# Last two expert blocks of a mixture-of-experts layer held in PSUM: sum rows added by identity products, normalised rows scattered to the outputs

## The reference, cut to what matters

```
def layer(x, ...):
    h = rmsnorm(x, g_mix); z = h @ w_in
    ...                                     # pool and retention branches
    x = x + mixed @ w_out
    h2 = rmsnorm(x, g_ffn)
    return x + hier_moe(h2, w_grp, w_exp, w1, w3, w2)

def hier_moe(h, ...):
    # a group of 8 experts by the largest group logit; in it the 2 best experts
    # weight = p_group * softmax of the two logits
    # per expert:  a = silu(xb @ w1[e]) * (xb @ w3[e]);  y = (a @ w2[e]) * weight
    # y is added to the row of its token

y_prompt, y_sample = rmsnorm(yp, g_final), rmsnorm(ys, g_final)
```

## Time and profile before

| | |
|---|---|
| Median of 3 runs | 1022.72 us (1022.17 to 1023.6) |
| The profiled execution | 1020.73 us, its span 1019.0 us |
| PE busy | 965.6 us (95%) |
| DVE, ACT, POOL busy | 740.3 us, 443.9 us, 219.4 us |
| Chain that ended last | PE 86%, DVE 6%, DMA 4% |
| First expert product, last expert product | at 684.0 us and at 987.5 us |

### The profile page before, as it was taken

The page is one execution under the profiler, slowest core; times in us unless marked ns, Lnnn a source line. Parts: engine busy times, 40 slices in busy tenths (PEclk is TensorE's granted clock), DMA queues, the critical chain, the costliest instruction groups (busy, mean ns, idle before and its releaser), DMA issues.

```text
span 1019.0 us, 16208 instructions
## 1 busy us (share of the span) xinstructions
PE 965.6 (95%) x5356; PEld 835.9 (82%) x5357; DVE 740.3 (73%) x1631; ACT 443.9 (44%) x739; POOL 219.4 (22%) x225
## 2 busy tenths in 40 slices
PE   6999999999999999999999999969999999999970
PEld 6998898988889888898886888857888888888860
DVE  5965466855678556685558666589999999999965
ACT  6621122121221212212113112148988998898864
POOL 0001220012200122001221100031443443443220
PEclk9999999999999999999999999979999999999995
DMA  9511105111051110512027332389999999999938
GB/s 317 179 42 54 42 22 176 40 53 39 25 173 41 54 34 29 173 33 80 35 81 261 150 140 103 117 310 408 394 393 393 391 401 388 392 395 382 340 50 333
DMA packets 74627, 190.21 MB, mean 187 GB/s; under 512 B 12519, under 2 KB 47443, under 8 KB 62131
## 3 DMA queue, kind: packets, MB, share of 16 engines
q1 hardware_dynamic: 61099, 159.07, 41.1%
q0 software_dynamic: 13312, 29.69, 9.9%
q10 hardware_dynamic: 144, 0.52, 0.2%
HBM read 167.43 MB, written 38.68 MB: 202 GB/s over the span
## 4 chain that ended last, share of the span: by engine, by line
PE 86%; DVE 6%; DMA 4%; ACT 1%; issue 1%; SPq 0%; POOL 0%; DVEq 0%; POOLq 0%; ACTq 0%
PE bank L2007 17%; PE bank L887 12%; PE bank L889 12%; PE bank L888 11%; PE bank L2008 9%; PE bank L918 8%; PE bank L1058 3%; PE bank L1996 1%; PE bank L958 1%; PE bank L2022 1%; PE bank L2030 1%; PE bank L2018 1%; PE bank L2026 1%; DVE x L1470 1%; DMA raw<-in_w_in_dram 1%
## 5 line engine op out<-in xcount | busy, mean ns | idle before, releaser
L1348 DVE TENSOR_TENSOR w_lo<-w,w_hi 128x1024 fp32r<-128x1024 f32 x128 | 150.3, 1216 | 0.1
L776 ACT ACTIVATE w_hi<-w 128x1024 fp32r<-128x1024 f32 x128 | 129.7, 1068 | 3.0 <-PE bank L889 2.9
L2007 PE MATMUL bank<-wvg_hi,hT_hi 128*128 128x512 f32 x256 | 104.4, 408 | 0.0
L887 PE MATMUL bank<-w_hi,xT_hi 128*128 128x512 f32 x256 | 102.9, 402 | 1.3 <-issue 1.3
L2007 PE MATMUL bank<-wvg_lo,hT_hi 128*128 128x512 f32 x256 | 100.9, 394 | 0.0
L2007 PE MATMUL bank<-wvg_hi,hT_lo 128*128 128x512 f32 x256 | 100.7, 393 | 0.0
L889 PE MATMUL bank<-w_hi,xT_lo 128*128 128x512 f32 x256 | 100.2, 391 | 0.0
L1814 ACT ACTIVATE v<-bank 128x256 f32<-128x256 f32 x32 | 12.3, 383 | 201.3 <-PE bank L2008 201.3
L888 PE MATMUL bank<-w_lo,xT_hi 128*128 128x512 f32 x256 | 99.7, 389 | 0.0
L2362 POOL TENSOR_TENSOR mixed<-onorm,pgate 128x256 f32<-128x256 f32 x36 | 38.9, 1080 | 272.4 <-DVE onorm L2178 272.4
L887 PE MATMUL bank<-hT_hi,wuqk_hi 128*128 128x344 f32 x288 | 94.1, 327 | 0.1
(11 more groups left out here) (279 smaller groups left out, 2390.3 us busy)
## 6 DMA issues: line engine op xcount, KB each, us to landing
w<-in_w_dram SPq DMA_DIRECT2D x96, 1024.0 KB
raw<-in_w_in_dram SPq DMA_DIRECT2D x57, 256.0 KB, 3.2
mixed_d<-mixed POOLq DMA_DIRECT2D x32, 128.0 KB, 2.1
sample_state<-in_state_ret_dram SPq DMA_DIRECT2D x16, 256.0 KB, 3.7
out_dram<-sample_state SPq DMA_DIRECT2D x16, 256.0 KB, 3.6
mixed_in<-mixed_d SPq DMA_DIRECT2D x8, 512.0 KB, 4.2
x_again<-in_x_prompt_dram SPq DMA_DIRECT2D x8, 512.0 KB, 3.4
h_d<-h POOLq DMA_DIRECT2D x8, 512.0 KB, 3.0
```

What stands on the lines that cost most here:

```text
L776: act.activation(hi, whole_w, ACT.Copy).then_inc(S["up_hi"], 1)
L887: pe.matmul(out, lhs[0], rhs[0], start=first, stop=False)
L1348: dve.tensor_tensor(lo, whole_w, hi, ALU.subtract).then_inc(S["up_lo"], 1)
L2007: g = pe.matmul(gates, x[xi], wvg[wi][:, 1:3, k, :], start=first, stop=last)
```

## The change

The y of blocks 30 and 31 is no more taken out and added in DRAM. For these two blocks the token's weight is multiplied in at the gate, and `down` leaves its sums open in the banks. `sum_d` needs the blocks 0 to 29 only (`SUMS` is 16 for each of 15 scatters on each of two semaphores). SP loads the tiles then, into a new buffer `fin` over weight slots that are free. POOL gathers from `sum_d` the rows of the tokens of blocks 31 and 30, and PE adds them to the banks by a product with the identity. The rows in the banks are final sums: ACT squares them and DVE scales them from there. They are a unit each, among the nine tiles, in `UNITS`. Tiles 8, 0, 1 and 2 are stored whole by SP; the prompt tiles 3 to 7 and both held units by POOL with indirect stores, in which the rows of a tile that belong to a held unit have an index out of range. A held unit has two stores, one for y_prompt and one for y_sample.

```
+        UNITS = [("tile", CH), ("tile", 0), ("tile", 1), ("tile", 2), ("tile", 3), ("held", NE - 1), ("tile", 4),
+                 ("held", NE - 2), ("tile", 5), ("tile", 6), ("tile", 7)]
+        PLAIN = 4
-        NORM_GROUPS = ((0, 3), (3, 6), (6, 8), (8, 9))
+        NORM_GROUPS = ((0, 2), (2, 5), (5, 8), (8, NU))
# SP
-            sp.wait_ge(S["parts_ready"], after(1))
+            for i in range(2):
+                sp.wait_ge(sum_out[i], SUMS)
             for n, t in enumerate(ORDER):
-                sp.dma_start(x2[r, t, :], sum_d[t * P:t * P + r.stop, :]).then_inc(rows_in[n], 16)
+                sp.dma_start(fin[r, t, :], sum_d[t * P:t * P + r.stop, :]).then_inc(rows_in[n], 16)
# ACT, step_m
                     sigmoid(b, s % 2)
+                    act.activation(small[:, EPSC + 1:EPSC + 2], small[:, EPSC:EPSC + 1], ACT.Sqrt)
                     a_high(b, s % 2)
-                    y_stored(b - 1, s - 1, g)
-                    y_out_of_psum(b - 1, (s - 1) % 2)
                     return
...
                 for q in range(DOWNS):
                     down_high(b, s % SLOTS, uses(s, g), q)
+                if isinstance(b, int) and b == NE - ROUND:
+                    many_act.append(spill_count(act))
# ACT, a held unit
+                    for q in range(2):
+                        act.wait_ge(S["z_mm"], after(2 * (NE - 1 - t) + q + 1))
+                        act.activation(junk_f[:, 0:512], down_bank(t, q), ACT.Square, scale=D ** -0.5, ...)
# PE, after down(31)
+            for b in range(NE - 1, NE - 1 - HELD, -1):
+                pe.wait_ge(xg_in[b % SLOTS], 16 * (MAIN_USES[b % SLOTS] + 1))
+                for n in range(2):
+                    pe.matmul(down_bank(b, n), ident, xg[b % SLOTS][:, n * 512:(n + 1) * 512], start=False, stop=True)\
+                        .then_inc(S["z_mm"], 1)
# DVE, gate
+                if is_held(b):
+                    dve.scalar_tensor_tensor(out=aa[s2][:, :], in0=banks[2 + s2][:, FE:2 * FE],
+                                             scalar=slot_w[:, b:b + 1], in1=sig[s2][:, :], op0=ALU.mult, op1=ALU.mult)
# DVE, at the end of step_m
+                if isinstance(b, int):
+                    store_rows(b - (NE - ROUND))
...
+            def store_rows(step):
+                if step == 0:
+                    spill_total()                      # the three instructions of L1403 to L1406
+                elif step == 1:
+                    many_dve.append(spill_count(dve))  # wait for spill_known, value_load
+                elif step == 2:
+                    ...                                # 3 instructions, 128x18 and 128x8
+                elif step == 3:
+                    ...                                # 3 instructions, 128x8
+                elif step == 4:
+                    ...                                # 2 instructions, 128x2
# POOL, after the scatter of block 29
+            for b in range(NE - 1, NE - 1 - HELD, -1):
+                pool.indirect_dma_start(out=xg[b % SLOTS][:, :], out_offset=None, in_=sum_d,
+                                        in_offset=indexed(idx_tok[:, b:b + 1]), ...)
+            for n, (kind, t) in enumerate(UNITS):
+                if n < PLAIN:
+                    continue
+                pool.wait_ge(S["y_done"], after(n + 1))
+                if kind == "tile":
+                    pool.indirect_dma_start(out=y_prompt[0], out_offset=indexed(row_store[:, t:t + 1]),
+                                            in_=fin[:, t, :], ...)
+                    continue
+                pool.wait_ge(y_out, 16 * PLAIN)
+                pool.indirect_dma_start(out=y_prompt[0], out_offset=indexed(idx_tok[:, t:t + 1]), in_=yb[i][:, :], ...)
+                pool.indirect_dma_start(out=y_sample..., out_offset=indexed(sample_store[:, i:i + 1]),
+                                        in_=yb[i][:, :], ...)
```

More of the change, by code:

```diff
@@ L343, in step_kernel @@
         junk_f = rc.place("junk_f", [P, D], F32)
+        ov_wide = rc.place("ov_wide", [P, NE, 8], F32)
+        over = rc.place("over", [P, 1], F32)
+        held = rc.place("held", [P, 2 * NT], F32)
+        held_rows = rc.place("held_rows", [P, CH], F32)
+        row_pair = rc.place("row_pair", [P, CH], I32)
+        row_store = rc.place("row_store", [P, CH], I32)
+        far = rc.place("far", [P, HELD], F32)
+        sample_store = rc.place("sample_store", [P, HELD], I32)
+        assert rc.at <= whole.end
+        fin = nc.alloc_sbuf_tensor_at("fin", [P, NT, D], F32, offset=at_W)
+        assert at_W + NT * D * 4 <= rm.where["w2_1"]
+        y_spill = nc.alloc_sbuf_tensor_at("y_spill", [P, D], F32, offset=ry.where["w2_hi_end"])
         SS, MS, RS = 0, 9, 18
@@ L851, in stage_c_act, with save_held, sqrt_again @@
             blocks(act, step_m)
-            y_stored(NE - 1, NE - 1 - ROUND * ROUNDS, ROUNDS)
-            y_out_of_psum(NE - 1, (NE - 1) % 2)
+            def save_held():
+                act.wait_ge(S["spill_mm"], after(1))
+                for i in range(2):
+                    act.wait_ge(sum_out[i], SUMS)
+                for i, b in enumerate(range(NE - HELD, NE)):
+                    for n in range(2):
+                        act.activation(yb[i][:, n * 512:(n + 1) * 512], down_bank(b, n), ACT.Copy)\
+                            .then_inc(S["y_ev"], 1)
+            def sqrt_again():
+                act.activation(small[:, EPSC + 1:EPSC + 2], small[:, EPSC:EPSC + 1], ACT.Sqrt)
             def more(b, i):
@@ L865, in more @@
                     down_high(b, 0, MAIN_USES[0] + i + 1, q)
[L866 to L878 removed]
+                act.wait_ge(sum_out[0], SUMS + 16 * (b - NE))
@@ new lines, in more, with root_of_units @@
+                y_out_of_psum(b, y_spill)
+            spilled(act, many_act[0], more, save_held, sqrt_again)
+            def root_of_units(a, b):
+                for n in range(a, b):
+                    if UNITS[n][0] == "held":
+                        act.wait_ge(S["mean_done"], after(NE - UNITS[n][1]))
+                return act.activation(small[:, MSF + a:MSF + b], small[:, SSF + a:SSF + b], ACT.Sqrt,
+                                      bias=small[:, EPSC:EPSC + 1])
+            squares = 0
@@ L1043, in spill_list @@
             def spill_list():
-                pe.wait_ge(S["spill_hot"], after(1))
+                pe.wait_ge(S["spill_hot"], after(2))
                 for i in range(2 * NT):
@@ L1477, in stage_c_dve @@
                     a, b = NORM_GROUPS[n]
-                    dve.wait_ge(S["root3_done"], after(n + 1))
-                    do(rsqrt_columns(steps, dve, *(small[:, at + a:at + b] for at in (SS, MS, HX, RS, TX))))
+                    for m in range(a, b):
+                        if UNITS[m][0] == "held":
+                            mean_of_halves(m)
+                    dve.wait_ge(S["root_done"], after(ROOT3 + n + 1))
+                    do(rsqrt_columns(steps, dve, *(small[:, at + a:at + b] for at in (SSF, MSF, HXF, RSF, TXF))))
                 else:
@@ L1540, in stage_c_pool @@
             blocks(pool, step_m)
-            for b in range(NE - SLOTS, NE):
+            for b in range(NE - SLOTS, NE - HELD):
                 scatter(b, b - ROUND * ROUNDS, ROUNDS, icol[b % ROUND][:, :])
@@ L1563, in _ @@
+            pool.wait_ge(rows_stored, 16 * stores)
         @block.sync
```

224 lines of the change are left out of this document (153 added, 71 removed).

## The result

| | before | changed |
|---|---|---|
| Median of 4 runs | 1022.44 us (1019.74 to 1023.6) | 1034.97 us (1033.67 to 1035.7) |
| The profiled execution, its span | 1020.73 us, 1019.0 us | 1035.7 us, 1033.9 us |
| Ratio, 95% interval | | 1.0122, 1.0102 to 1.0142 |

The account below looks back on a forecast made before the run. PE was taken to bound the blocks, a chain through POOL, SP, ACT and DVE the end. Loads 8.1 us sooner, 4.8 more until DVE's end, 5.5 more after: 2.2 us slower, 1024.9 us; range 1022.5 to 1027.5, 8 in 10 1019.5 to 1030.0.

Parts of the forecast that it names:

- Step 1: Step 24: ACT waits for DVE's spill count, 0.5 us to read it; PE 2.65 us late.
- Step 2: Steps 25 to 28: DVE's count read and small instructions bring PE's lag to 3.55 us, taken as 3.6.
- Step 3: Step 31: table load and its activation, 1.28 + 0.20 us, fit in ACT's 2.02 us wait, without a 1.38 us drain.
- Step 4: Start of SP's loads: after block 29's scatter lands, 4.24 us from its start, at 985.7, 8.1 us sooner.
- Step 5: Gathers land in 8.9 us; PE idles four us, then does four products of 1.5 us at or near 1.2 GHz.
- rival C: Gathered rows early: quiet-queue landing in 4.42 us, PE at its higher level, ACT never waits; 1023.5 us, chance 0.12.
- step 6: ACT and DVE at the end: first load to DVE's end takes 27.0 us against 22.2, DVE done at 1012.7.
- Step 7: POOL's eight indirect stores: first at 1006.3, 1.5 us apart, last at 1016.8, landing 4.2 us later, end 1021.2.
- rival A: POOL's stores spaced like the accumulating one: 1.9 us apart gives 1027.7 us, 2.75 gives 1033.7; chance 0.20.
- rival D: POOL keeps up: y_sample stores almost free, others 1.29 us apart, end at 1017.9; 1021.6 us, chance 0.18.

Follow-up runs that it names:

- a1: Changed kernel without POOL's drain at the end of the block: 1026.11 us, ratio 1.0049 to the kernel before.
- a5: Changed kernel, PE filling its wait in step 25 with three idle float32 products of 256 columns: 1033.05 us in one run.
- after_again: Changed kernel once more, unedited: 1036.34 us, ratio 1.0133 to the kernel before.
- a2: Changed kernel with ACT's read of the spill count moved from step 24 to behind its last step: 1030.71 us, ratio 1.0088.
- best3: best1 with POOL's drain at the end kept and another between its gathers and stores: 1019.96 us, ratio 0.9975 to the kernel before.
- a3: a2 with DVE's additions spread over seven steps ahead of down_low, and DVE's count read behind its last step: 1028.11 us, ratio 1.0067.
- best2: best1 with the held units fourth and sixth and SP storing three tiles whole: 1022.21 us, ratio 0.9995 to the kernel before.
- best1: Changed kernel with the edits of a3 and a1, both y_sample stores last: 1018.45 us, ratio 0.9964 to the kernel before.
- a4: Changed kernel with a second POOL drain between its landed gathers and its stores: 1027.49 us in one run.

## Why the prediction was right and wrong, step by step

The direction came out for reasons that were half of the case. The path was seen: the stall in step 24, POOL as the last engine, the spacing of its stores. The end of the program was not. The direction didn't hang on the drain that was overlooked: without it, in a1, the changed kernel is still 4.4 us slower than before (1026.11 against 1021.75 beside it), though that is twice the 2.2 of the forecast.

- **Step 1, mis-sized.** The first two intervals grew by 4.98 us (12.04 + 11.71 against 9.40 + 9.37), predicted 2.65. Reading the count took 1.16 and not 0.5 us, and a clock fall of 1.7 us wasn't foreseen. I had put the read between 0 and 0.55 by a gap on ACT ahead of the table load. But there the value had been ready since 986.25, and ACT's sequencer had loaded it beside the last y, before that gap began at 988.60. The views of the line that reads it, before and then changed:

```profile
L594 ACTq TENSOR_LOAD <-spill x1: 487/487/487, 987.9 to 987.9; - x1
L594 ACTq SEQ_ASSERT  x1: 29/29/29, 988.6 to 988.6; - x1
```

```profile
L609 ACTq TENSOR_LOAD <-spill x1: 486/486/486, 928.9 to 928.9; - x1
L609 ACTq SEQ_ASSERT  x1: 29/29/29, 929.9 to 929.9; - x1
```

In step 24 nothing hides the load, from 928.9 on.
- **Step 2, right.** The other four intervals grew by 1.1 us (38.63 against 37.53), predicted 0.9.
- **Step 3, right.** The table load lies in ACT's wait for PE, with no drain of its own:

```profile
991.40 1.28 ACT L850 ACT_TABLE_LOAD   x1
...
992.69 0.20 ACT L850 ACTIVATE small<-small 128x1 f32<-128x1 f32 x1
...
993.50 0.39 ACT L829 ACTIVATE aT_hi<-bank 128x256 fp32r<-128x256 f32 x1 [0.61 <-PE bank L1130]
```

`sig` ended at 991.38 and the load began at 991.40, as in the earlier trace rows. The drain of 1.38 us that the Trainium skill has in ScalarE: Activation LUTs, What ACT_TABLE_LOAD costs, isn't there for the second time.
- **Step 4, 7.2 us late.** 3.6 of it came from ahead of the y of block 23, 2.5 from steps 1 and 2, and 1.2 from block 29's scatter, which had landed for SP 5.45 us after its start at 987.46 and not 4.24, the value of the last one of before.
- **Step 5, wrong, to the good.** The gathers landed in 5.9 to 7.3 us and not 8.9, between the bounds. PE was idle only from 997.6, for 1.76 us and not for 4, and still at clock 1.00: a pair of products took 1.99 us, not 3.

```profile
DMA to landing us min/median/max: 5.9/6.6/7.3
```

```profile
999.33 1.99 PE L1201 MATMUL bank<-xg,misc 128*128 128x512 f32 x4 [1.76 <-DMA xg<-sum_d,idx_tok]
1002.05 1.99 PE L1201 MATMUL bank<-xg,misc 128*128 128x512 f32 x4 [0.74 <-DMA xg<-sum_d,idx_tok]
```

ACT squared held 31 at 1004.24 without a wait for PE. That is rival C's mechanism (the rows there before ACT needs them, PE at its higher level), though not its quiet queues: the landings lie between its 4.42 us and the 8.9 of the forecast. Of the 27.0 us of step 6 some 1.2 were the wait for PE, which can account for the 1.1 us that this stretch was shorter.
- **Step 6, right but for that.** DVE's end came 25.9 us after the first load.
- **Step 7, right in the spacing, 0.7 us off in the start.** The spacing was 1.28 us (predicted 1.5, rival A 1.9 to 2.75), and POOL's first held store started 1.5 us after DVE had scaled that unit (1011.86 to 1013.36; predicted 0.8). The 0.7 us between are the wait for SP's four plain stores, which was to cost nothing: POOL's sequencer came past that wait (L1713) at 1012.5, and SP, which waits for the same stores, at 1012.5 too.

```profile
L1713 POOLq EVENT_SEMAPHORE  x2: 17/17/17, 1012.5 to 1014.2; - x2
L188 SPq COMPARE_BRANCH  x1: 38/38/38, 1012.5 to 1012.5; - x1
```

The timeline puts this idle time down to DVE, but in every kernel with this order of units (a1 to a5, after_again) the store starts 0.8 to 0.9 us after that wait, and 1.4 to 2.0 after DVE. A plain indirect store costs what a gather costs, and one with nearly all indices out of range costs the same 0.98 us, which ends rival D.
- **The failing step was the last line of step 7**, "and lands after 4.2 us as the last scatter did: 1021.0, end 1021.2". I carried the 0.2 us of the end over from a program in which POOL had been done 25 us before, and looked at no row of POOL after its last DMA. That row was there to see in the trace of before (8.28 us). With it the forecast would have been 1024.9 + 7 = 1032 us, 3 below the measured 1034.97. In a1, without the drain, the span is 1024.2 where the sum said 1021.2. Those 3.0 us are 2.4 from steps 1 and 2 and 1.3 from block 29's scatter, less 0.8 in the end; there the start was as before (919.46).

The Trainium skill (VectorE: DVE Perf Modes, The DRAIN you can't avoid) has the drains that the runtime puts into its pre- and postamble at a constant 12 ns or so on all engines. The drains here are those at the end of the program's own block, of which it doesn't speak. SP's 7 ns is of that size; POOL's 6.93 us is nearly 600 times as long, so the figure is no guide to it, and the measurement decides.

## What to carry to other kernels

An engine's last instruction isn't its last cost: before you move the end of a kernel to another engine, read what its sequencer does behind its list, and for GpSimd expect a drain of several microseconds once it has issued many DMAs (here 6.9 to 8.3 us after 120 and more, 0.8 after nine). Let another engine end the kernel, or drain GpSimd once in a wait that it has anyway. And a read of a just computed value into a register is a wait on a chain across engines: put it behind the last step or where the engine stands idle, and put small work ahead of a wait that its engine has anyway.

## What the runs showed of the hardware that I had not expected

- POOL's drain goes with the number of DMAs that POOL issued since its last one: 0.785 us after 9, 3.17 after 38, 6.76 after 82, about 0.08 us each. After 120 it is 8.28 us, at once or 25.5 us later, and after 129 it is 6.93.
- From the end of the CAST on DVE until ACT's next instruction it was 1.16 us, for the semaphore and the read into a register (no branch stands there).
- Plain indirect stores of up to 128 rows are busy 0.98 us on POOL and follow each other in 1.28 us, whether few or nearly all rows have an index out of range. One of each kernel's, the fourth or fifth, is busy for 1.2 to 2.0 us, and why no run shows. The accumulating one is busy 1.55 to 1.6 us. They land in 2.1 us (nearly nothing to write), 2.6 to 2.9 (held rows) and 3.3 to 3.7 us (tiles).
- PE's clock fell to 0.50 behind a stall of 2.66 us and also behind one of 1.44 us, with PE busy again, and once, at 427.5, behind a wait of 1.71 us on the memory of the samples' state, in code that the change doesn't touch. Ahead of the products with the identity it stayed at 1.00 with waits of 1.76 us (changed kernel), 2.21 (a2) and 2.23 (best3), and fell with 2.27 (a3), 2.50 (best2) and 3.02 (best1). The falls in step 25 and those at 172, 427.5 and 550 lasted 3.4 us each, the one of a4 6.8.
